# Value stage of a decoder step: later row sums, activations in two loads, long runs in DRAM, and the first group prepared a stage early

## What is computed

```python
idx, gate = top 16 of 256 candidates, per token and head   # 8 heads
act = gelu(einsum('thkd,td->thk', u_tab[idx], hb))         # key stage
y   = einsum('thk,thkd->td', gate * act, v_tab[idx])       # value stage
x   = x + y;  y_out = rmsnorm(x, g_final)
```

## Time and profile before

| what | value |
|---|---|
| median of 3 runs | 3577.66 us (3575.85 to 3577.73) |
| the profiled execution | 3571.98 us, of which the span is 3570.2 us |
| PE busy | 3331.6 us, 93% |
| POOL busy | 2319.5 us, 65% |
| DVE busy | 2276.9 us, 64% |
| ACT busy | 1109.2 us, 31% |
| DMA | 970.34 MB, mean 272 GB/s |
| key stage, dense units | about 1293 to 2407 us of the span |
| value stage | about 2418 to 3545 us, then 25 us of closing work |

### The profile page before, as it was taken

The page is one execution under the profiler, slowest core; times in us unless marked ns, Lnnn a source line. Parts: engine busy times, 40 slices in busy tenths (PEclk is TensorE's granted clock), DMA queues, the critical chain, the costliest instruction groups (busy, mean ns, idle before and its releaser), DMA issues. The chain is left out here.

```text
span 3570.2 us, 58151 instructions
## 1 busy us (share of the span) xinstructions
PE 3331.6 (93%) x22639; PEld 3149.4 (88%) x22639; DVE 2276.9 (64%) x4059; ACT 1109.2 (31%) x1531; POOL 2319.5 (65%) x1923
## 2 busy tenths in 40 slices
PE   7999987889998999999999999998999989998997
PEld 6988853547998999999999999998999989998997
DVE  7832224325215999986797766565678768877764
ACT  4111132343223233444444444322222222222232
POOL 2533307003443448888888888886888888878873
PEclk9999989999999999999999999999999999999998
DMA  4597978672322235888889888888987888888862
GB/s 162 190 364 308 353 270 283 222 263 92 143 103 88 83 117 198 319 328 345 338 321 353 330 340 343 340 310 302 351 332 304 340 345 323 308 341 344 320 265 90
DMA packets 251661, 970.34 MB, mean 272 GB/s; under 512 B 44673, under 2 KB 108802, under 8 KB 172930
## 3 DMA queue, kind: packets, MB, share of 16 engines
q1 hardware_dynamic: 151394, 553.25, 42.2%
q0 software_dynamic: 57344, 335.58, 23.5%
q10 hardware_dynamic: 42720, 78.87, 6.0%
HBM read 891.32 MB, written 73.92 MB: 270 GB/s over the span
## 5 line engine op out<-in xcount | busy, mean ns | idle before, releaser
L129 POOL TENSOR_TENSOR wl<-raw,wh 128x512 fp32r<-128x512 f32 x776 | 1053.0, 1390 | 638.5 <-ACT wh L122 637.3
L122 ACT ACTIVATE wh<-raw 128x1024 fp32r<-128x1024 f32 x396 | 397.5, 1051 | 1229.3 <-PE acc L1563 602.8
L1935 PE MATMUL acc<-vh,wh 128*128 128x360 f32 x2048 | 683.9, 334 | 89.4 <-DVE xt L2014 69.4
L1867 POOL TENSOR_TENSOR wl<-raw,wh 128x512 fp32r<-128x512 f32 x504 | 649.8, 1324 | 130.7 <-ACT wh L1905 128.7
L1561 PE MATMUL acc<-hh,wh 128*128 128x360 f32 x2048 | 677.4, 331 | 8.2 <-POOL wl L129 8.1
L1937 PE MATMUL acc<-vh,wl 128*128 128x360 f32 x2048 | 682.0, 333 | 0.0
L1936 PE MATMUL acc<-vl,wh 128*128 128x360 f32 x2048 | 681.2, 333 | 0.0
L1563 PE MATMUL acc<-hh,wl 128*128 128x360 f32 x2048 | 671.0, 328 | 0.0
L1562 PE MATMUL acc<-hl,wh 128*128 128x360 f32 x2048 | 670.8, 328 | 0.0
L147 PE MATMUL acc<-hh,wh 128*128 128x256 f32 (+1 forms) x1920 | 546.2, 285 | 7.3 <-DVE tt L427 4.7
L148 PE MATMUL acc<-hl,wh 128*128 128x256 f32 (+1 forms) x1920 | 543.5, 283 | 0.0
(11 more groups left out here) (363 smaller groups left out, 4973.7 us busy)
## 6 DMA issues: line engine op xcount, KB each, us to landing
raw<-units SPq DMA_DIRECT2D x324, 1024.0 KB, 5.2
kr<-cache_k SPq DMA_DIRECT2D x128, 512.0 KB, 6.5
vr<-cache_v SPq DMA_DIRECT2D x128, 512.0 KB, 5.9
expert_acts<-ast ACTq DMA_DIRECT2D x128, 180.0 KB
expert_gates<-gs ACTq DMA_DIRECT2D x15, 1536.0 KB, 7.5
a<-expert_acts SPq DMA_DIRECT2D x16, 1440.0 KB, 18.4
g<-expert_gates SPq DMA_DIRECT2D x16, 1440.0 KB, 11.2
output_steps<-qo ACTq DMA_DIRECT2D x16, 288.0 KB, 7.4
```

The lines of the kernel that those rows point to most:

```text
L122: act.activation(m.wh[s][:, k:k + KT // 2, :], m.raw[s][:, k:k + KT // 2, :], ACT.Copy).then_inc(m.hi_done, 1)
L129: x = pool.tensor_tensor(m.wl[s][:, part, :], m.raw[s][:, part, :], m.wh[s][:, part, :].bitcast(F32), ALU.subtract)
L1867: x = pool.tensor_tensor(wl[v % RW][:, part, :], raw[v % RW][:, part, :], wh[v % RW][:, part, :].bitcast(F32), ALU.subtract)
L1935: pe.matmul(tile_acc[r % AW], wh[b][:, VT * e + d, :], vh[g % 2][:, e, :], start=(e == 0), stop=False)
```

## The change

It has five parts.

1. **Rows.** Row sums come one unit later in DVE's order and the gathers one unit earlier in POOL's. The narrow rows likewise. Between a gather and its sum lie three units instead of one, with the same four buffers.
2. **Preparation.** `NQ` is 2 instead of 4: each group's activations are weighed, rounded and subtracted in two pieces of 1440 columns (units 2 and 3 for `weigh`, 4 and 5 for `low`) instead of four of 720. These pieces now stand directly behind the add of tile 1, ahead of the narrow rows.
3. **Loads.** The activations come in two loads behind units 4 and 5 of a group. The gates are loaded behind unit 3, for which SP waits only until the previous group's gates are used.
4. **DRAM layout.** `m.aD` and `m.gD` put the partition first. What a partition loads is one run: 5760 bytes of activations, 11520 bytes of gates. The 15 stores of gates go out in runs of 768 bytes instead of 12288.
5. **First group.** Its activations and gates are loaded behind the load of key unit 117. DVE weighs them in unit 120, ACT rounds them in unit 121, DVE subtracts in unit 122, each as 8 instructions of 360 columns. `first_vh` gets a place of its own, and the value stage starts without these steps.

`y_sb` is also copied one unit later.

```diff
-RW, AW, NQ = 3, 3, 4
+RW, AW, NQ = 3, 3, 2
+E_FIRST = 116
...
# stage_e, SP
-            with sp.Fori(0, (N_PQ + N_EXP) // 2) as i:
+            with sp.Fori(0, (N_PQ + E_FIRST) // 2) as i:
...
-            sp.dma_start(m.first_acts[:, :, :], m.aD[0:GRP, :, :].rearrange("e p n -> p e n")).then_inc(m.first_acts_in, 16)
+            sp.dma_start(m.first_acts[:, :, :], m.aD[:, 0:GRP, :]).then_inc(m.first_acts_in, 16)
             sp.wait_ge(S["gates_stored"], 16 * NB)
-            sp.dma_start(..., m.gD[:, :, 0:GRP, :].rearrange("b p e n -> p b (e n)")).then_inc(m.gates_in, 16)
+            sp.dma_start(..., m.gD[:, 0, :, :]).then_inc(m.gates_in, 16)
+            for e in range(E_FIRST, N_EXP):
+                load_unit(m, sp, U_EXP_U + e + 2, e % 2)
...
# stage_e, ACT
-                        act.dma_start(m.gD[blk, :, :, :]..., gs[blk % 2]...)
+                        act.dma_start(m.gD[:, :, blk, :], gs[blk % 2][:, :, :].rearrange("p (g e) n -> p g (e n)", g=NG))
+                if e == E_FIRST + 5:
+                    for x in range(GRP):
+                        act.wait_ge(m.first_weighed, x + 1)
+                        act.activation(m.first_vh[:, x, :], m.first_acts[:, x, :], ACT.Copy).then_inc(m.first_hi, 1)
...
# stage_e, DVE
+                if e == E_FIRST + 4:
+                    dve.wait_ge(m.first_acts_in, 16)
+                    dve.wait_ge(m.gates_in, 16)
+                    for x in range(GRP):
+                        a = m.first_acts[:, x, :].rearrange("p (b n) -> p b n", b=NB)
+                        dve.tensor_tensor(a, a, m.gates[:, :, x, :], ALU.mult).then_inc(m.first_weighed, 1)
+                if e == E_FIRST + 6:
+                    for x in range(GRP):
+                        dve.wait_ge(m.first_hi, x + 1)
+                        dve.tensor_tensor(m.first_vl[:, x, :], m.first_acts[:, x, :], m.first_vh[:, x, :].bitcast(F32), ALU.subtract)
...
# rows before and after
-sums_by (j - 2), rows_by (j - 1), sums_x_by (j - 3), rows_x_by (j - 2)
+sums_by (j - 3), rows_by (j),     sums_x_by (j - 4), rows_x_by (j - 1)      # each * 9 // 8, between 0 and HK
...
# stage_f, SP
-                if n == (2 if g == 0 else 1) and g + 1 < NG:
-                    sp.wait_ge(S["weighed"], GRP * g + GRP)
-                    sp.dma_start(m.gates..., m.gD[:, :, GRP * g + GRP:GRP * g + 2 * GRP, :]...)
-                if n == 4 and g + 1 < NG:
+                if n == 3 and g + 1 < NG:
                     if g > 0:
+                        sp.wait_ge(S["weighed"], GRP * g)
+                    sp.dma_start(m.gates..., m.gD[:, g + 1, :, :]).then_inc(m.gates_in, 16)
+                if 4 <= n < 4 + NQ and g + 1 < NG:
+                    if g > 0 and n == 4:
                         sp.wait_ge(S["tile_done"], UPG * VT * g)
-                    sp.dma_start(a4[(g + 1) % 2][:, :, :], m.aD[GRP * g + GRP:GRP * g + 2 * GRP, :, :]...)
+                    e0 = GRP * (g + 1) + GRP // NQ * (n - 4)
+                    sp.dma_start(a4[(g + 1) % 2][:, parts[n - 4], :], m.aD[:, e0:e0 + GRP // NQ, :]).then_inc(ain[n - 4], 16)
...
# stage_f, DVE
                         dve.tensor_tensor(x, x, tile_acc[r % AW], ALU.add).then_inc(S["sum_added"], 1)
+                        if d == 1 and g + 1 < NG and 2 <= n < 2 + NQ:
+                            weigh(g + 1, n - 2)
+                        if d == 1 and g + 1 < NG and 4 <= n < 4 + NQ:
+                            low(g + 1, n - 4)
...
-                        if d == 1 and g + 1 < NG and 2 <= n < 2 + NQ:
-                            weigh(g + 1, n - 2)
-                        if d == 1 and g + 1 < NG and 3 <= n < 3 + NQ:
-                            low(g + 1, n - 3)
```

More of the change, by code:

```diff
@@ L1371, in stage_e @@
     m.first_acts = at("a40", [P, GRP, ND], off=first); m.gates = at("g8", [P, NB, GRP, BW], off=first + GRP * ND * 4)
-    m.first_end = first + 2 * GRP * ND * 4
+    m.first_vh = at("vh0", [P, GRP, ND], F32R, off=first + 2 * GRP * ND * 4); m.first_vl = at("vl0", [P, GRP, ND], F32R, off=first)
+    m.first_end = first + 3 * GRP * ND * 4
     assert m.first_end <= m.top
@@ L1821, in stage_f @@
     yx = m.acc[:, 1, 0, :]
-    S = {n: sem("g_" + n) for n in "ain1 raw2_in weighed weighed_hi weighed_lo sum_added tile_done rows_added y_kept y_turned squares_ready squares_added squares_summed root_ready out_ready out_stored x_added x_turned".split()}
+    S = {n: sem("g_" + n) for n in "raw2_in weighed weighed_hi weighed_lo sum_added tile_done rows_added y_kept y_turned squares_ready squares_added squares_summed root_ready out_ready out_stored x_added x_turned".split()}
     raw_in = m.raw_in + [S["raw2_in"]]
-    ain, x_in = [m.first_acts_in, S["ain1"]], [sem(f"g_x_in{n}") for n in range(4)]
+    ain, x_in = [sem(f"g_ain{q}") for q in range(NQ)], [sem(f"g_x_in{n}") for n in range(4)]
     vg_in = [sem(f"g_vgin{j}") for j in range(GW)]
@@ L1886, in w_hi @@
                 act.activation(vh[g % 2][:, parts[q], :], a4[g % 2][:, parts[q], :], ACT.Copy).then_inc(S["weighed_hi"], GRP // NQ)
-            for e in range(GRP):
-                act.wait_ge(S["weighed"], e + 1)
-                act.activation(vh[0][:, e, :], a4[0][:, e, :], ACT.Copy).then_inc(S["weighed_hi"], 1)
             for n in range(1, 4):
@@ L1908, in _ @@
                     w_hi(g + 1, n - 3)
-                if v == N_EXP - UPG:
+                if v == N_EXP - UPG + 1:
                     act.wait_ge(S["rows_added"], HK)
@@ L1932, in _ @@
                     for e in range(GRP):
-                        if n == 0 and d == 0:
-                            pe.wait_ge(S["weighed_lo"], GRP * g + e + 1)
+                        if g > 0 and n == 0 and d == 0 and e % (GRP // NQ) == 0:
+                            pe.wait_ge(S["weighed_lo"], GRP * (g - 1) + e + GRP // NQ)
                         pe.matmul(tile_acc[r % AW], wh[b][:, VT * e + d, :], vh[g % 2][:, e, :], start=(e == 0), stop=False)
@@ L1987, in add_square @@
                     dve.tensor_tensor(rs[:, :], rs[:, :], sq[:, k % 4, :], ALU.add).then_inc(S["squares_added"], 1)
-            dve.wait_ge(ain[0], 16)
-            dve.wait_ge(m.gates_in, 16)
-            for e in range(GRP):
-                a = a4[0][:, e, :].rearrange("p (b n) -> p b n", b=NB)
-                dve.tensor_tensor(a, a, m.gates[:, :, e, :], ALU.mult).then_inc(S["weighed"], 1)
-                if e > 0:
-                    first_low(e - 1)
-            first_low(GRP - 1)
             for g in range(NG):
```

40 lines of the change are left out of this document (18 added, 22 removed).

## The result

The changed kernel takes 3532.09 us (median of 4 runs, 3521.92 to 3537.37). Beside it, in the same rounds, the kernel before took 3576.76. The ratio is 0.987, with an interval of 0.985 to 0.990: 45 us faster. The forecast was 95 us faster, and the time lies above the top of its range. The direction was right, the size was half. Of all the runs in this document one, a run of `both_nq4` that took 8283.68 us, was slow; it is left out of the numbers.

The account below looks back on a forecast made before the run. PE bounds the key stage; a loop over SP, DMA, POOL and DVE, none full, delays the value stage. 83.7 + 9.5 + 2.2 + 1.8 - 2 = 95.2 us off 3571.98 gives 3476.8; 5.7 above, 3482.5 us (3471 to 3490, chance 0.60).

Parts of the forecast that it names:

- Preparation in two pieces: Value stage: half as many DVE pieces, each 1.8 to 6.9 us, inside PE's 7.9 us cover; cost nothing, at most 2.7.
- residue: Value-stage period beyond PE's 63.2 us: between 0 and 2.7 us, taken as 0.8, so 64.0 a period, gain 83.7 us.
- POOL is the bound: Rival: POOL's splits and gathers set the value-stage period at today's disturbed 65.9 us; 3510 us, chance 0.15.
- Key stage: Two loads (2.9 MB) and 16 DVE instructions in its last units cost 2 us, between 0 and 10.
- Rows: Value stage: three units (23.7 us) between gather and sum remove the gather wait that PE's idle stretch ends with.
- New wait on POOL: Value stage: 4 of 9 gathers wait for rows summed in the same unit; POOL loses 0.7 of 9.7 us, costed nothing.
- Start of the value stage: Ahead of the periods: pacing and two idle stretches go, a 2.4 us wait for unit 2 stays; gain 9.5 us.
- Border: Last key matmul to first value matmul: the first value matmul moves to where a weighing began; gain 1.8 us.
- DRAM layout: Long load runs give no DMA time back, short stores cost the key stage none: 0, bounds -5 and +15 us.
- Memory rate: Rival: memory sustains only 337 GB/s, value-stage period 68.6 us; 3549 us, chance 0.05.
- milder memory rival: Memory at a core's share of about 358 GB/s, value-stage period 64.6 us; 3491 us, chance 0.15.
- End of the stage: Behind the value stage's periods: the slow matmuls of one stretch go, gain 2.2 us; the later `y_sb` copy costs nothing.

Follow-up runs that it names:

- both_nq4: Changed kernel with first-group loads spread, its subtractions after the last dot product, four 720-column pieces, and DVE making a quarter of each POOL split: 3456.57 us, ratio 0.968.
- late_pieces: Changed kernel with DVE's weighing and subtraction pieces moved behind the narrow rows: 3523.81 us, ratio 0.986.
- old_layout: Changed kernel with the DRAM layout, stores and loads of the kernel before (part 4 undone): 3534.54 us, ratio 0.991.
- key_lows: Changed kernel with only the first group's eight DVE subtractions moved behind the last dot product, loads left together: 3509.28 us, ratio 0.982.
- key_both: Changed kernel with first-group loads in four parts behind units 112, 114, 116, 118 and its subtractions behind the last dot products: 3502.21 us, ratio 0.980.
- no_first: Changed kernel without part 5: first group loaded behind the last key unit and weighed at the value stage's start: 3498.17 us, ratio 0.979.
- rows_only: Kernel before with part 1 alone (later sums, earlier gathers) and the later `y_sb` copy: 3486.37 us, ratio 0.976.
- nq4: Changed kernel with preparation in four pieces of 720 columns and activations in four loads: 3486.36 us, ratio 0.976.
- prep_on_act: Changed kernel without weighing, ACT making a second copy instead of DVE's subtraction, so the result is not the layer's: 3474.36 us, ratio 0.973.
- both: Changed kernel with first-group loads spread, its subtractions after the last dot product, two long pieces, and DVE making a quarter of each POOL split: 3458.14 us, ratio 0.969.

## Why the prediction was right or wrong

**The period: the step "Preparation in two pieces" failed.** It costed the longer pieces at "Nothing, with an upper end inside the 2.7 above". Measured, a period is 67.2 us, 4.0 above PE's 63.2 and not the 0.8 that I took. I read the earlier trace rows, where DVE waits for a split, as the whole of the collision. (They show the subtractions alone; the weighings of the kernel before already had a median of 3.37 us.) The other collision was not looked for: POOL's gather issue under DVE's piece. A gather that is issued under a piece doesn't pay a share of the overlap; it ends 0.8 us behind the piece, however short its own work. Undisturbed, a unit of POOL takes 7.42 us from split to split (POOL's timeline of the changed kernel, units without a piece):

```profile
2696.57 5.03 POOL L1887 TENSOR_TENSOR wl<-raw,wh 128x512 fp32r<-128x512 f32 x4
2701.76 0.96 POOL L1892 DMA_INDIRECT vg<-expert_v,idx  x1 [0.16 <-issue]
2703.02 0.95 POOL L1897 DMA_INDIRECT vgx<-expert_v,idxx  x1 [0.31 <-issue]
2703.99 5.02 POOL L1887 TENSOR_TENSOR wl<-raw,wh 128x512 fp32r<-128x512 f32 x4
```

Eight of those and two more gathers at 1.26 make 61.9 us. Adding what the nine `vg` and nine `vgx` of a group take above their bare 0.96 and 0.95 gives the measured period within 0.6 us in every kernel in which POOL is the bound (means of the value stage; periods as the mean of 13):

| kernel | mean `vg`, `vgx` us | 61.9 + extra | measured period |
|---|---|---|---|
| changed kernel | 1.401, 1.087 | 67.1 | 67.2 |
| late_pieces | 1.508, 0.950 | 66.8 | 66.85 |
| old_layout | 1.487, 0.948 | 66.6 | 66.8 |
| key_lows | 1.217, 1.117 | 65.7 | 65.9 |
| key_both | 1.146, 1.137 | 65.3 | 65.6 |
| no_first | 1.035, 1.160 | 64.5 | 65.0 |
| rows_only | 1.224, 0.947 | 64.3 | 64.3 |
| nq4 | 0.993, 1.154 | 64.0 | 64.0 |
| prep_on_act | 0.955, 0.949 | 61.9 | 63.04, PE |

So my 64.0 is what four short pieces give (nq4), and near what the earlier trace rows would have given by this sum: 61.9 + 9 x 0.227 = 63.9. The residue (what a period takes beyond PE's 63.2 us) was right for the old pieces and was carried over to the new ones. The rival "POOL is the bound" named the right engine for another reason, late DVE work. That its 65.9 us came nearer to 67.2 than my number was luck in part: its sum used the mean of 1.324 us of subtractions that overlap. Their busy time by their count is 1.289, and with it the sum is 64.8.

The Trainium skill (SBUF — State Buffer, "Who interferes with whom") has a DVE `tensor_tensor` with both inputs in SBUF contend with GpSimd's reads, but reports a probe in which it did not stall DMA, and infers as the reason that descriptor generation needs the ports' write interface. By that rule the pieces would have cost the gathers nothing; here an issue is stretched from 0.96 to 2.39 us beside such an instruction, and the measurement decides. A gather also reads its row numbers (`idx`) from SBUF; whether that read is what waits, no run here shows.

**Two phases.** With long pieces the same code ran at 64.6 us a period (no_first, part of key_both) and at 67.2 (the changed kernel, part of key_both). In the first the pieces begin about half a microsecond into `vg` and only `vgx` pays, at 1.5 to 1.8 us. In the second three of a group's four pieces begin just before `vg` and one just before `vgx`, which then take 2.2 to 2.4. A loop could hold the second: the stretched gather makes the next split late, PE waits for it for half a microsecond, DVE's add of tile 1 falls earlier against POOL's split, and the next piece meets `vg` again. But such a loop is not shown. The changed kernel keeps to about 67.2 in all 13 periods and no_first to 64.6 in eleven; in key_both the two are mixed, and in the first eight periods of key_lows they alternate. What puts a group in one or the other stays open; no run was made for it. The extra gain of `key_both` beyond its 13 us, and the miss at `no_first`, go with the shorter periods.

**Key stage: right in kind, mis-sized.** I took 2 us with 10 as the bound, and it is 13.6 (10.5 to 16.6 in the other kernels with both causes). I priced the 16 DVE instructions by how long they could hold POOL off, and the loads inside the same bound, though I had counted their 2.9 MB and knew from the value stage that `raw` queues behind such loads. What the runs show instead: the loads hold `raw` up, a PE stretch of 4 to 9 us (key_lows leaves only this one), and the subtractions hold up DVE's rows, for which POOL waits, a stretch of 3.9 us (gone in key_lows); slow matmuls follow both. With both causes gone the term is 0.4 us (key_both). I had covered DVE's own time by the 21.61 us of the earlier trace rows, but that wait comes at the end, and the subtractions came ahead of rows that POOL needs.

**Right.** Rows: DVE's waits for gathers went from 245.8 to 1.6 us, and rows_only shows that this part carries the gain. New wait on POOL: 6.3 us in all in the changed kernel. Start of the value stage: 9.6 us gained against 9.5, with a wait for unit 2 of 1.61 against 2.4. Border: 1.8. DRAM layout: nothing either way in the whole time (old_layout), with the short runs' one open place as said there. Memory rate: no bound, since `both` moved 357 GB/s with PE full. The Trainium skill (HBM Reference, "Specifications (TRN2)") says that a core which streams alone measures well above its share of about 358 GB/s; the 403 GB/s of the earlier trace rows agree, and my milder memory rival rested on the share.

**End of the stage.** The 2.2 us of slow matmuls came back as one stretch of 2.57 us behind DVE's adds at 3421.09. The timelines of DVE and POOL point to a cause:

```profile
3406.87 12.21 DVE L1977 TENSOR_TENSOR a<-a,g 128x1440 f32<-128x1440 f32 x1
3407.53 10.04 POOL L1887 TENSOR_TENSOR wl<-raw,wh 128x512 fp32r<-128x512 f32 x8
```

The gathers have run out, so POOL makes two splits with nothing between them, and a weighing of 1.65 us lasts 12.21, until 1.5 us behind the second. The next tile add stands behind it. The traces of nq4, no_first, key_both and key_lows have the same pair, a weighing of 11.2 to 12.1 us and a stretch of about 2.5 on PE. The prediction's "1.8 to 6.9 us" for a long piece missed this case.

## What to carry to other kernels

When an engine that only just keeps up lies next to the bound (here POOL at 61.9 us beside PE's 63.0), price what its neighbours' instructions do to every kind of instruction it runs, the DMA issues too; a DVE instruction of 1.65 us with two SBUF inputs made a gather of 0.96 us last up to 2.4. In a stage in which PE is busy for 99.9%, put added loads in small parts between the stream's own, and put DVE's added work behind whatever another engine waits for: so placed it cost 0.4 us (key_both), and otherwise 13.6. And time the parts of a change one by one: here part 1 alone gave 87 us, and the other four took 42 of it back. Nearly all of that is part 2, since with short pieces (nq4) the other parts leave the ratio of part 1 alone, 0.976, as it is.

## What the runs showed of the hardware

- A POOL gather issued under a running DVE `tensor_tensor` on SBUF inputs ends 0.81 to 0.84 us after that instruction: 2.39, 2.20 and 1.71 us instead of 0.96, for pieces of 1.65 us. What counts is which of the two begins first: in key_both every gather whose piece began 0.04 us or more ahead of it took 1.49 to 2.44 us, and every one whose piece began later than that stayed at 0.94 to 0.96. DVE instructions with an operand in PSUM stretch none (120 gathers in the changed kernel, 0.94 to 0.97).
- A DVE `tensor_tensor` on SBUF inputs that begins inside a run of POOL's subtractions waits out the run: 4 to 7 us for 1.65 of work behind one split (late_pieces), 12.21 behind two.
- The same instructions ran at 64.6 and at 67.2 us a period, in one trace too (key_both, key_lows), by a shift of a few tenths of a microsecond between two engines.
- 357 GB/s over 978 us at a DMA share of 0.89, with PE never short of data.
- Short runs cost packets, not time: from 1490 to 2266 us ACT's queue (packets, MB, share of 16 engines) went from the first line, before, to the second, the changed kernel, and PE's busy time there stayed.

```profile
q10 hardware_dynamic: 14688, 38.25, 12.5%
```

```profile
q10 hardware_dynamic: 41568, 38.25, 14.7%
```
